# Transposing the local attention's probabilities by DMA instead of on TensorE, in a hybrid decoder layer

## The reference, cut to what matters

```
proj = h @ w_in                                    # 256 x 3088, cut into qa ka va | qg kg vg rg | glr
# group A: 8 heads of width 64; with 256 tokens there is one block, so this is causal attention
s = qa @ ka.T * 64**-0.5 - slope[h] * distance     # masked above the diagonal
p = softmax(s)
o = p @ va                                         # (256 x 256) @ (256 x 64) for each head
# group B: gated linear attention on qg, kg, vg with decays from glr, gated by silu(rg)
mix = concat(o, gla_o) @ w_mix_o
x = LN1(alpha * x + mix)
x = LN2(alpha * x + CrossAttn(x, mem))             # k, v = mem @ w_xkv
x = LN3(alpha * x + relu(x @ w_ff1)**2 @ w_ff2)
```

## Time and profile before

| | |
|---|---|
| median of 3 runs | 395.91 us (395.84 to 396.65) |
| span of the profiled execution, first to last instruction | 394.0 us |
| TensorE busy | 387.7 us, 98% |
| VectorE busy | 347.4 us, 88% |
| ScalarE busy | 263.6 us, 67% |
| GpSimd busy | 80.4 us, 20% |
| mean granted TensorE clock | 0.998 of full |

### The profile page before, as it was taken

One profiled execution on the slowest core, in us unless ns is written; L12 is line 12 of the kernel. 1 busy time (PEld: TensorE's weight loads), 2 busy tenths in 40 slices (PEclk: granted clock), 3 DMA queues, 4 the chain that ended last, 5 costly groups with the idle time before them and its releaser, 6 DMA issues.

```text
span 394.0 us, 5663 instructions
## 1 busy us (share of the span) xinstructions
PE 387.7 (98%) x2092; PEld 330.7 (84%) x2092; DVE 347.4 (88%) x450; ACT 263.6 (67%) x349; POOL 80.4 (20%) x79
## 2 busy tenths in 40 slices
PE   8999999999999999999999999999999999999995
PEld 5888888888988888889988888888888888888883
DVE  5699595899989786969798898999999999999997
ACT  6666568756554638447683658888888777788741
POOL 2049400037870204000004300000000000000003
PEclk9999999999999999999999999999999999999999
DMA  8997737743656181563637464777777678677102
GB/s 286 378 385 265 248 119 256 244 162 113 221 200 215 54 302 73 213 213 115 235 120 306 135 216 134 235 236 232 210 249 220 216 229 240 229 234 218 31 2 106
DMA packets 25313, 79.70 MB, mean 202 GB/s; under 512 B 1766, under 2 KB 3398, under 8 KB 21190
## 3 DMA queue, kind: packets, MB, share of 16 engines
q1 hardware_dynamic: 22448, 74.81, 54.5%
q0 software_dynamic: 2160, 3.93, 5.7%
q10 hardware_dynamic: 678, 0.59, 0.5%
HBM read 78.28 MB, written 1.05 MB: 201 GB/s over the span
## 4 chain that ended last, share of the span: by engine, by line
PE 96%; DVE 2%; DMA 1%; issue 0%; ACT 0%; DVEq 0%
PE bank L1671 17%; PE bank L1672 16%; PE bank L1673 16%; PE bank L2056 13%; PE bank L1730 13%; PE bank L1734 7%; PE bank L2063 7%; PE bank L1882 2%; PE bank L1677 1%; DMA raw<-in_lead 1%; PE bank L1836 1%; DVE X L1625 1%; PE bank L1869 0%; DVE stats L1616 0%; PE bank L1935 0%; PE bank L1984 0%
## 5 line engine op out<-in xcount | busy, mean ns | idle before, releaser
L1076 DVE TENSOR_TENSOR w_lo<-raw,w_hi 128x2048 fp32r<-128x2048 f32 x30 | 70.6, 2359 | 6.9 <-ACT w_hi L650 6.9
L650 ACT CAST w_hi<-raw 128x2048 fp32r<-128x2048 f32 x32 | 60.7, 1912 | 13.0 <-PE bank L1673 11.1
L2056 PE MATMUL bank<-actA,w_hi 128*128 128x512 f32 x224 | 55.4, 390 | 0.0
L2056 PEld LDWEIGHTS bank<-actA,w_hi 128*128 128x128 f32 x224 | 42.0, 188 | 8.7
L613 POOL DMA_DIRECT2D raw<-in_w_ff x15 | 13.1, 877 | 155.8 <-DMA raw<-in_w_ff 155.8
L1671 PE MATMUL bank<-w_hi,actB 128*128 128x512 f32 x107 | 42.6, 398 | 0.0
L1672 PE MATMUL bank<-w_lo,actB 128*128 128x512 f32 x107 | 41.8, 391 | 0.0
L1673 PE MATMUL bank<-w_hi,actB 128*128 128x512 f32 x107 | 41.8, 390 | 0.0
L1730 PE MATMUL bank<-actA,w_hi 128*128 128x512 f32 x156 | 38.3, 392 | 0.0
L1671 PE MATMUL bank<-w_hi,actA 128*128 128x512 f32 x96 | 38.0, 396 | 0.0
L1673 PE MATMUL bank<-w_hi,actA 128*128 128x512 f32 x96 | 37.5, 390 | 0.0
(11 more groups left out here) (255 smaller groups left out, 870.0 us busy)
## 6 DMA issues: line engine op xcount, KB each, us to landing
raw<-in_w_ff SPq DMA_DIRECT2D x32, 1024.0 KB, 5.6
raw<-in_w_in SPq DMA_DIRECT2D x10, 1024.0 KB, 7.1
raw<-in_w_xkv SPq DMA_DIRECT2D x8, 1024.0 KB, 5.1
raw<-in_w_mix_o SPq DMA_DIRECT2D x4, 1024.0 KB, 4.9
raw<-in_w_xq SPq DMA_DIRECT2D x4, 1024.0 KB, 5.0
raw<-in_w_xo SPq DMA_DIRECT2D x4, 1024.0 KB, 5.0
raw<-in_w_ff POOLq DMA_DIRECT2D x15, 256.0 KB, 5.2
raw<-in_lead SPq DMA_DIRECT2D x6, 384.0 KB, 5.1
```

What stands on the lines that cost most here:

```text
L650: act.copy(dst, half_view(u)).then_inc(hi_done, 1)
L1076: dve.tensor_tensor(dst, half_view(u), hi_part.bitcast(f32), ALU.subtract).then_inc(lo_done, 1)
L2056: pe.matmul(b[:, :].rearrange("p (h s) -> p h s", h=2), hi[:, k, m * P:(m + 1) * P], actA[:, :, k, :], start=k == 0, stop=False, skip_grou ...
```

## The change

The 24 TensorE transposes and ScalarE's eight copies of their results are gone. For each pair of heads (four pairs, 768 float32 columns each) GpSimd copies the probabilities as 16-bit words into `probsT`, the low words of a head in one plane of 384 and the high words in another (`make_planes`). SyncE's queue then transposes the twelve 128x128 blocks of 16-bit words back into `probs` (`turn_planes`), and GpSimd joins the words to float32 in `probsT` (`join_planes`). TensorE's `pv` products stand behind the first two memory keys `xk00` and `xk01` and wait for all four joins. VectorE's and ScalarE's lists are rearranged around them, and the bank table with them.

```diff
-    + [(f"pt{h}", 4 + h) for h in range(4)] + [("rg0", 2)] + [(f"pt{h}", h) for h in range(4, 8)]
-    + [("diag", 0), ("rg1", 3), ("pv0", 4), ("pv1", 5), ("xk00", 0), ("xk01", 1)]
+    + [("rg0", 2), ("diag", 0), ("rg1", 3), ("xk00", 0), ("xk01", 1), ("pv0", 6), ("pv1", 7)]
...
+        pair_words = [v[:, 768 * j:768 * (j + 1)].bitcast(u16) for v in (probs, probsT) for j in range(HA // 2)]
+        probs_words, planes = pair_words[0:4], pair_words[4:8]
+        def by_word(v):
+            return v.rearrange("p (h n x) -> p h x n", h=2, x=2)
+        def by_plane(v):
+            return v.rearrange("p (h x n) -> p h x n", h=2, x=2)
...
 SyncE
-            load_chunk(6)
+            def turn_planes(j):
+                sp.wait_ge(planes_made, j + 1)
+                sp.dma_start(probs_words[j].rearrange("p (g q) -> p g q", q=P), planes[j], transpose=True)\
+                    .then_inc(turned_in[j], 16)
+            load(unit(6, 0), chunk_source(6, 0), 4)
+            turn_planes(0)
+            load(unit(6, 1), chunk_source(6, 1), 4)
+            turn_planes(1)
             sp.dma_start(X[:], x.rearrange("(t p) n -> p t n", p=P)).then_inc(x_in, 16)
-            load_chunk(7)
+            turn_planes(2)
+            load(unit(7, 0), chunk_source(7, 0), 4)
+            turn_planes(3)
+            load(unit(7, 1), chunk_source(7, 1), 4)
...
 GpSimd
+            def make_planes(j):
+                pool.wait_ge(prob_done, 4 * (j + 1))
+                pool.tensor_copy(by_plane(planes[j]), by_word(probs_words[j])).then_inc(planes_made, 1)
+            def join_planes(j):
+                pool.wait_ge(turned_in[j], 16)
+                pool.tensor_copy(by_word(planes[j]), by_plane(probs_words[j])).then_inc(probsT_made, 1)
+            make_planes(0)
+            make_planes(1)
+            join_planes(0)
+            join_planes(1)
+            make_planes(2)
+            make_planes(3)
             wait_full(pool, "diag")
             pool.memset(lev_q[1], 0.0).then_inc(lev_q_zeroed, 1)
+            join_planes(2)
+            join_planes(3)
...
 ScalarE
-            for h in range(4):
-                transposed(h)
...
-            for h in range(4, 8):
-                transposed(h)
...
             hi_half(6, 1)
-            exp_r(1)
-            mix(0, "pv0")
-            mix(1, "pv1")
...
             decay(0)
+            exp_r(1)
             hi_half(7, 0)
             decay(1)
+            hi_half(7, 1)
+            act.wait_ge(probsT_made, 2)
             memk(0, 0)
-            hi_half(7, 1)
             memk(0, 1)
+            mix(0, "pv0")
+            mix(1, "pv1")
...
 VectorE
             lo_half(6, 0)
+            lo_half(6, 1)
             silu(0)
             exponents(1)
-            lo_half(6, 1)
+            silu(1)
+            exponents(2)
             mix(0, "pv0")
             mix(1, "pv1")
-            silu(1)
-            exponents(2)
...
 TensorE
-            for h in range(4):
-                transpose_probs(h)
             tokens(5, 0, A, "rg0")
-            for h in range(4, 8):
-                transpose_probs(h)
...
             two_blocks(6, 0, ["xk00", "xk01"], actB)
+            for name in ["va0", "va1"]:
+                wait_out(pe, name)
+            pe.wait_ge(probsT_made, HA // 2)
+            for n in range(2):
+                b = begin(f"pv{n}")
+                ...
             level(0)
             level(1)
```

More of the change, by code:

```diff
@@ L193, in build @@
           w_xo, ln2_g, ln2_b, w_ff1, w_ff2, ln3_g, ln3_b, consts, out):
-    f32, f32r, i32 = mybir.dt.float32, mybir.dt.float32r, mybir.dt.int32
+    f32, f32r, i32, u16 = mybir.dt.float32, mybir.dt.float32r, mybir.dt.int32, mybir.dt.uint16
     ALU, ACT, AX = mybir.AluOpType, mybir.ActivationFunctionType, mybir.AxisListType
@@ L358, in build @@
         bias_done, score_done, exp_done, prob_done = map(sem, ("bias_done", "score_done", "exp_done", "prob_done"))
+        planes_made, probsT_made = sem("planes_made"), sem("probsT_made")
+        turned_in = [sem(f"turned_in{j}") for j in range(HA // 2)]
         mix_hi = sem("mix_hi")
@@ L713, in exps @@
                                    accum_out=sums[:, 2 * h + t:2 * h + t + 1]).then_inc(exp_done, 1)
-            def transposed(h):
-                b = wait_full(act, f"pt{h}")
-                act.copy(probsT[:, h * 384:(h + 1) * 384], b[:, 0:384]).then_inc(freed(f"pt{h}"), 1)
             hi_half(4, 0)
@@ L1829, in score @@
                     .then_inc(full(f"score{h}"), 1)
[L1831 to L1837, removed]
             tokens(3, 0, A, "va0")
@@ L1861, in _ @@
             tokens(5, 1, A, "rg1")
[L1862 to L1873, removed]
             def level(n):
@@ L1911, in _ @@
             two_blocks(6, 0, ["xk00", "xk01"], actB)
+            for name in ["va0", "va1"]:
[3 more added lines that the diff above has]
+                b = begin(f"pv{n}")
+                for h in range(4 * n, 4 * n + 4):
+                    r = slice(64 * (h % 2), 64 * (h % 2) + 64)
+                    c = (h // 2 - 2 * n) * S
+                    pe.matmul(b[r, c:c + S], va[:, 0, h * DA:(h + 1) * DA], probsT[:, h * 384:h * 384 + S],
+                              start=True, stop=False)
+                    i = pe.matmul(b[r, c + P:c + S], va[:, 1, h * DA:(h + 1) * DA],
+                                  probsT[:, h * 384 + S:h * 384 + 384], start=False, stop=True)
+                i.then_inc(full(f"pv{n}"), 1)
             level(0)
```

## The result

The kernel after the change takes 400.73 us (median of 4 runs, 399.95 to 400.9) against 396.27 (4 runs, 395.84 to 396.65) for the kernel before on the same chip: a ratio of 1.0106, 95% interval [1.0088, 1.0125]. It is slower by 4.5 us.

What follows compares the result with a forecast made beforehand. TensorE, never waiting around the change, was taken to bound the kernel. Gain -2.8, wait ahead of pv +3.9, wait at level 1 +2.3 sum to +3.4: span 394.0 becomes 397.4, median 1.9 above, 399.3 us; range 393.0 to 411.0.

Steps and rivals of the forecast that it cites:

- The gain: On TensorE, transposes removed (2.6 us) and pv products moved: 2.8 us gained if nothing else happened.
- the moved products: On TensorE, pv behind the memory keys means one change of product kind fewer: 0.1 to 0.2 us gained.
- The price of a copy: Each GpSimd copy of 1536 words per partition takes 2.4 us, between 1.4 and 4.7, sized from a subtraction.
- The price of a transpose: Each transposing DMA on SyncE's queue lands 4.1 us after issue, 2.0 for its data; bounds 3.2 and 11.
- My chain: Copies, transposes, queue and VectorE subtractions step by step: last transpose lands at about 84, join 3 ends at 87.1 us.
- The rival of dear transposes: Two transposes in sequence in the chain, each 7 us dearer, add 14 us: 413 us; chance 0.14.
- The wait ahead of the product: TensorE waits ahead of pv for GpSimd's last join, from 83.2 to 87.1 us: 3.9 us.
- The wait ahead of level 1: TensorE waits 2.3 us for level 1's operands, since VectorE's exponents 1 end late, at 90.0 us.
- up to 1 us may hide there: Later levels and VectorE subtractions (7,0), (7,1) come as late as TensorE: nothing added, up to 1 us possible.
- The clock: Rival: TensorE's clock falls behind the wait, 3 to 4 us of work doubles, 402 to 403; counted in the forecast's range.
- joins in time: Rival: copies at 1.4 us, transposes at 3.2, join 3 near 81, before the 83.2 deadline: 393.2 us; chance 0.24.
- Dear copies: Rival: GpSimd copies at 4.7 us each, four of them in the chain add 9.2 us: 408.5 us; chance 0.15.

Runs made afterwards that it cites:

- no_words: Kernel after without 16-bit copies and transposing DMAs; the product reads what already stands in probsT, so the transposition is left out: 393.6 us, ratio 0.9937.
- no_copies: Kernel after without the eight GpSimd copies; the four transposing DMAs stay, carry zeros and go out once their heads are normalised: 393.5 us, ratio 0.9937.
- pv_moved: Kernel before, TensorE transposes kept, with pv behind the first two memory keys and VectorE's and ScalarE's lists in the new order: 396.07 us, ratio 0.9997.
- no_turn: Kernel after without the four transposing DMAs; all eight GpSimd copies stay and joins read the words as they were: 400.08 us, ratio 1.0105.
- planes_first: Kernel after with GpSimd's splits 2 and 3 ahead of join 1: 400.97 us, ratio 1.0122.
- both: Kernel after with VectorE's exponents 1 ahead of silu 0 and GpSimd's splits 2 and 3 ahead of join 1: 402.49 us, ratio 1.0159.
- both_act: The kernel of both, with the first two splits on ScalarE instead of GpSimd: 402.12 us, ratio 1.015.
- act_eight: Kernel after with all eight copies (splits and joins) on ScalarE, none on GpSimd: 398.47 us, ratio 1.0052.
- late_join: Kernel after with splits and joins 2 and 3 on ScalarE, two casts ahead of its splits, GpSimd's join 1 behind level 0's operands: 395.04 us, ratio 0.9968.
- late_swap: The kernel of late_join with VectorE's subtraction (7,1) ahead of exponents 3: 396.27 us, ratio 0.9999.

## Why the prediction was right, point by point

The forecast was 399.3 us with a range of 393.0 to 411.0, slower with a chance of 0.71. Measured are 400.73. The sign and the mechanism held, several sizes did not, and the account of what causes the first wait is wrong in one part.

**The gain** was forecast at 2.8: it is 2.7 by the timeline, 2.5 by no_words and no_copies. The part of it given to the moved products, 0.1 to 0.2, is below what pv_moved can tell.

**The price of a copy** was forecast at 2.4 us: it is 1.5 for a split and 1.9 for a join where nothing holds them. I sized it from a subtraction; the memset of the earlier trace rows at 0.94 ns an element was much nearer (the split comes to 0.98, the join to 1.2). That copies lengthen beside VectorE's operations was right, but to 3.46 to 4.00 where I had 4 to 5.

**The price of a transpose** was forecast at 4.1 us to landing: it is 3.7 at its shortest, with nothing ahead of it in the queue. That one moved its data from about 76.3 to 78.4 us at some 180 to 220 GB/s, where the load behind it reached 330 to 430: its data took the 2.0 us that I had put down for them. Where a load stands ahead of it in the queue it was 6.9 to 7.6, and the last one, on which join 3 waits to 84.60, took 7.1 from its issue at 77.48. My chain had it land at 84, behind the load (7,0), and so it was. The Trainium skill, "VectorE: DVE Perf Modes", The three transpose paths, has 1309 ns for one 128x128 block by DMA; twelve blocks came in 3.7 us, so its figure doesn't add up block by block. The rival of dear transposes (413) is refuted.

**The wait ahead of the product**: forecast 3.9 us from 83.2 to 87.1, measured 2.1, from 84.7 to 86.7; join 3 ends at 86.5 where I had 87.1. The wait's start was later by 1.5 for what came before it: 0.8 at the start of the kernel, and 0.44 and a restart at the low halves of (6,1).

**The wait ahead of level 1**: forecast 2.3, measured 1.5; exponents 1 ended at 89.1 instead of 90.0.

**What was missed**: waits for the subtractions of (6,1) and (7,1), 0.44 and 0.73 us. Of (7,0) and (7,1) the prediction said that "up to 1 us may hide there", and with the restart it was that. For (6,1) there is no term, though the chain itself has this subtraction end at 84.7, behind the time at which TensorE asks for it (about 81.6 by the prediction's start of the keys at 77.5, an estimate from the 4.1 us that it takes from the start of the keys to these products without a wait): most of the forecast wait should have stood there. The overlap lost at the restarts, estimated above at 1.1, was in no term.

**Luck**: the two waits that were forecast came out 2.6 us smaller (3.6 for 6.2), the missed ones and the restarts added 2.3, and the late start 0.8. That the time came within 1.4 us of the forecast rests on these cancelling.

**The step that failed** is what the chain was taken for. In the kernel after the first wait does end as forecast: GpSimd idles 3.77 us until the last transpose has landed at 84.60, and join 3 ends at 86.5. But I added the wait as a price of that chain, in which copies, transposes and queue each have their part. The runs show that taking the chain's links away doesn't give the time back: without the DMAs (no_turn) the kernel is as slow, with join 3 earlier (planes_first) too, and with the DMAs and without copies (no_copies) it has the full gain. What costs is that GpSimd's copies and VectorE's operations exclude each other while VectorE has no slack: 5.8 us of lateness, which TensorE meets at whichever product depends on the end of VectorE's list. The prediction had this mechanism from the earlier trace rows and used it within the chain, but not as the one account on which all waits draw. Hence also my wrong expectations for `both` and `both_act`. What the DMAs cost while the copies stay is not separated, since leaving them out also moves the copies: from the subtraction at 53 us to `silu` 0 VectorE takes 29.8 us in no_turn, 29.1 in after and 23.3 in no_copies. The Trainium skill, "SBUF — State Buffer", Who interferes with whom, states that where VectorE and GpSimd need the ports that they share, the one that comes second is blocked for the whole instruction of the first; this trace agrees (0.23 us of copy became 1.37, and 1.9 in no_turn).

**The clock** did not fall in the profiled execution of after: 1.00 in every 3 us from 83 to 101, behind waits of 2.1 and 1.5. It fell in no_turn and act_eight behind waits of 3.2 and 2.4, and cost 1.6 us in no_turn, half of what the rival said (3 to 4). The three other executions of after are 0.8 to 1.1 us longer than the profiled one, with mean clocks of 0.993 and 0.994 against 0.997. That it is the same fall is not shown, since they have no trace; in act_eight the executions with a mean clock of 0.999 and 1.000 (398.18 to 398.63) are hardly shorter than those with 0.993 (398.38 to 398.75).

**The rivals**: "joins in time" did not come about (join 3 at 86.5), though the copies' own price came near its condition of 1.4 us. The prediction named a copy near 1.4 as a sign that the kernel gets faster; a split took 1.5, and the kernel got slower, since copies were held and the last transpose took 7.1. "Dear copies" is refuted by 1.5 and 1.9 us.

## What to carry to other kernels

An engine with idle time is not a free place for work: what a GpSimd copy cost here is the time that it took from a VectorE with no slack, and it was paid at whichever product waited for the end of VectorE's list. If removing one wait by another order makes the next one grow by as much, the cause is a shared lateness, and only less work, or work beside operations that it doesn't exclude (here a reciprocal, or another engine), gets the time back. A DMA with a long way to landing costs nothing while its data are wanted later than that, as in no_copies; test it alone before putting it on the chain.

## What the runs showed of the hardware beyond that

- GpSimd's copy of 1536 16-bit words per partition takes 1.50 us when it reads with a step (split) and 1.9 when it writes with one (join); ScalarE takes 1.47 and 1.95 for the same.
- VectorE's copies with one SBUF input are held too (0.23 became 1.37 us in after), while a reciprocal of one input (3.35 us) ran at its full speed beside a join of 1.98 in late_join and of 1.89 in after.
- A transposing DMA holds SyncE's queue for 1.4 to 3.7 us at its issue (2.4 to 4.5 in no_copies), where the load (6,1) holds it for 0.37.
- The length of a single wait does not tell whether the granted clock falls. It stayed at 1.00 behind 2.1 us in after, and from 95 to 101 us behind 2.3 us in both_act; it was 0.67 to 0.76 behind 3.2 (no_turn) and 2.4 us (act_eight), 0.50 behind 2.25 us (planes_first), and 0.58 from 104 to 107 us behind 2.05 us in both_act.
- The same work at the start of the kernel can end up to 2 us later in one execution than in another: late_swap's profiled run has its first split at 55.19, late_join's at 53.14, and their lists are the same up to there. So single spans of such variants are not to be compared.
